# Order of the softmax steps in the attention loops: the copy of the turned probabilities moves between an item's maximum and its reciprocal

## The reference

```python
s = jnp.einsum("bhqd,bhkd->bhqk", q, k).astype(jnp.float32) * scale
if sink is not None:
    s = jnp.concatenate([s, sink_col], axis=-1)
p = softmax_f32(s)            # "swa" drops the sink's column behind it
return jnp.einsum("bhqk,bhkd->bhqd", p.astype(v.dtype), v)
```

## Time and profile before

| | |
|---|---|
| median of three runs | 4626.8 us |
| the profiled execution's own time | 4630.47 us |
| its span | 4628.6 us |
| TensorE matmuls busy | 3098.1 us (67%) |
| VectorE busy | 3119.4 us (67%) |
| ScalarE busy | 908.7 us (20%) |
| GpSimd busy | 1507.9 us (33%) |
| mean granted TensorE clock | 0.828 of full speed |

### The profile page before, as it was taken

The page is one execution under the profiler, slowest core; times in us unless marked ns, Lnnn a source line. Parts: engine busy times, 40 slices in busy tenths (PEclk is TensorE's granted clock), DMA queues, the critical chain, the costliest instruction groups (busy, mean ns, idle before and its releaser), DMA issues.

```text
span 4628.6 us, 49133 instructions
## 1 busy us (share of the span) xinstructions
PE 3098.1 (67%) x16352; PEld 1197.2 (26%) x16352; DVE 3119.4 (67%) x8343; ACT 908.7 (20%) x2468; POOL 1507.9 (33%) x1378
## 2 busy tenths in 40 slices
PE   6889898656885544555575787778885555445554
PEld 2455454311321111111121222554431111111111
DVE  1251346878777788777878764634687877877886
ACT  1252312111111111112111111541111111111211
POOL 0000112444434444444443432010344444344443
PEclk8999999978997787777797998997997777777776
DMA  4252315999999999999999997122899999999998
GB/s 142 84 183 73 132 69 232 415 413 405 417 417 395 419 414 404 420 415 403 393 418 404 415 395 272 35 87 77 333 406 403 408 419 411 408 419 411 398 417 341
DMA packets 307838, 1518.48 MB, mean 328 GB/s; under 512 B 26144, under 2 KB 94240, under 8 KB 143744
## 3 DMA queue, kind: packets, MB, share of 16 engines
q0 software_dynamic: 185888, 1347.13, 70.8%
q1 hardware_dynamic: 87616, 133.07, 8.3%
q10 hardware_dynamic: 34080, 35.14, 2.2%
HBM read 1499.03 MB, written 16.20 MB: 327 GB/s over the span
## 4 chain that ended last, share of the span: by engine, by line
DVE 41%; PE 27%; DMA 19%; issue 7%; ACT 4%; POOL 1%; DVEq 1%; SPq 0%; ACTq 0%; POOLq 0%
DMA X<-in_uv_dram,X 17%; DVE X L2018 17%; PE ps L1112 7%; PE ps L579 6%; DVE X L2029 2%; ACT X L1563 2%; DVE X L1919 1%; DVE X L1917 1%; DVE X L1920 1%; DVE X L2025 1%; PE ps L1029 1%; PE ps L1095 1%; PE ps L906 1%; PE ps L794 1%; PE ps L823 1%
## 5 line engine op out<-in xcount | busy, mean ns | idle before, releaser
L1112 PE MATMUL ps<-X 64*64 64x512 f32 x2560 | 1621.3, 766 | 1276.7 <-DVE X L2029 1259.4
L2152 POOL DMA_INDIRECT X<-in_uv_dram,X x1280 | 1426.8, 1115 | 2166.3 <-PE ps L1115 1692.1
L2018 DVE CUSTOM_DVE_ANT_0 X<-yT,X 128x1024 f32<-128x1024 f32 x1280 | 1531.7, 1223 | 319.0 <-DMA X<-in_uv_dram,X 273.6
L1115 PE MATMUL ps<-X 64*64 64x512 f32 x2560 | 1621.6, 766 | 0.0
L1113 PE MATMUL ps<-X 64*64 64x512 f32 x2560 | 1621.5, 766 | 0.0
L1114 PE MATMUL ps<-X 64*64 64x512 f32 x2560 | 1621.5, 766 | 0.0
L1112 PEld LDWEIGHTS ps<-X 64*64 64x64 f32 x2560 | 355.9, 161 | 2444.1 <-DVE X L2029 1752.2
L1563 ACT ACTIVATE X<-X 128x1 f32<-128x1 f32 x1280 | 256.6, 202 | 2282.7 <-DVE X L2018 2224.3
L1115 PEld LDWEIGHTS ps<-X 64*64 64x64 f32 x2560 | 356.3, 161 | 0.0
L1113 PEld LDWEIGHTS ps<-X 64*64 64x64 f32 x2560 | 356.2, 161 | 0.0
L1114 PEld LDWEIGHTS ps<-X 64*64 64x64 f32 x2560 | 356.0, 161 | 0.0
(11 more groups left out here) (288 smaller groups left out, 3597.5 us busy)
## 6 DMA issues: line engine op xcount, KB each, us to landing
wring<-in_ada_w_dram SPq DMA_DIRECT2D x48, 1024.0 KB
wring<-in_w_in_dram SPq DMA_DIRECT2D x36, 1024.0 KB
wring<-in_peer_wq_dram SPq DMA_DIRECT2D x24, 1024.0 KB
X<-in_uv_dram,X POOLq DMA_INDIRECT x1280
wring<-in_w_out_dram SPq DMA_DIRECT2D x8, 1024.0 KB
X<-scores ACTq DMA_DIRECT2D x64, 128.0 KB
X<-mods ACTq DMA_DIRECT2D x15, 512.0 KB, 6.7
ahead<-X ACTq DMA_DIRECT2D x18, 256.0 KB
```

The costliest lines, as they stand in the source:

```text
L1112: pe.matmul(ps[0:HD, h, :], dg(slice(0, HD), s), v0[0:HD], **ends)
L1115: m = pe.matmul(ps[0:HD, 2 + h, :], dg(slice(HD, P), s + 1), v1[HD:P], **ends)
L2018: v.tensor_tensor_reduce(uvr[:, slot, 0:D], h2[:, t, :], uvr[:, slot, 0:D], 1.0, 0.0, ALU.mult, ALU.add, adot[:, s_:s_ + 1]).then_inc(S("d ...
L2152: g.indirect_dma_start(uvr[:, slot, :], None, a["uv"], bass.IndirectOffsetOnAxis(ap=istages[i % 2][:, s:s + 1], axis=0)).then_inc(S(f"uv{s ...
```

## The change

On ScalarE the normalisation that stands behind the exponential of item i is now that of item i itself. On VectorE the reciprocal of a round is now that of item i, too, and it stands behind the copy of item i-2. No instruction is added or taken away, and TensorE's, SyncE's and GpSimd's lists stay as they are.

```diff
@@ ScalarE, attention(kind)
                                                  bias=att[:, 1, c:c + 1], accum_out=att[:, 2, c:c + 1]).then_inc(S("a_exp"), 1)
-                        if 1 <= i <= N:
-                            j = i - 1
-                            w = width(items[j][2])
-                            act.wait_ge(S("a_r"), ab + j + 1)
-                            nc.scalar.activation(pr3[:, j % 3, 0:w], pr3[:, j % 3, 0:w], ACT.Copy, scale=att[:, 5, j % 32:j % 32 + 1]).then_inc(S("a_no"), 1)
+                            act.wait_ge(S("a_r"), ab + i + 1)
+                            nc.scalar.activation(pr3[:, i % 3, 0:w], pr3[:, i % 3, 0:w], ACT.Copy, scale=att[:, 5, c:c + 1]).then_inc(S("a_no"), 1)
                         p = (i - 5) // 2
                         if i >= 5 and i % 2:
                             y_out(p)
@@ VectorE, attention(kind)
-                        if 1 <= i <= N:
-                            c = (i - 1) % 32
-                            total = att[:, 2, c:c + 1]
-                            v.wait_ge(S("a_exp"), ab + i)
-                            if kind == "swa":
-                                link(v.tensor_tensor(att[:, 4, c:c + 1], att[:, 2, c:c + 1], att[:, 3, c:c + 1], ALU.add))
-                                total = att[:, 4, c:c + 1]
-                            v.reciprocal(att[:, 5, c:c + 1], total).then_inc(S("a_r"), 1)
                         if i >= 2:
                             j = i - 2
                             w = width(items[j][2])
...
                             v.tensor_copy(pT4[:, j % 4, 0:w], ps[:, 4:6, :].rearrange("p a b -> p (a b)")[:, 0:w]).then_inc(S("a_pt"), 1)
+                        if i < N:
+                            c = i % 32
+                            total = att[:, 2, c:c + 1]
+                            v.wait_ge(S("a_exp"), ab + i + 1)
+                            if kind == "swa":
+                                link(v.tensor_tensor(att[:, 4, c:c + 1], att[:, 2, c:c + 1], att[:, 3, c:c + 1], ALU.add))
+                                total = att[:, 4, c:c + 1]
+                            v.reciprocal(att[:, 5, c:c + 1], total).then_inc(S("a_r"), 1)
```

## The result

The changed kernel took 4663.2 us (median of four runs, 4657.1 to 4669.15), the kernel before beside it 4628.4 us (four runs). The ratio is 1.0071, with an interval of 1.0058 to 1.0083: slower by 0.7%, or 34.8 us, where the prediction said 22.6. A second measurement of the same text gave 4658.2 us, a ratio of 1.0068 (1.0054 to 1.0081). The direction and the two ties came out as told; the size lay above the range, at the upper end of rival 3 (22.6 + 6 to 12 us).

A forecast was written before the change was run, and what follows sets the result against it. Chains of waits bound the attentions, with TensorE mostly busy only in "mla". Terms of 12.5 us in layer 0 and 10.1 in layer 1 gave 22.6, added to the median 4626.8: 4649 us, range 4639 to 4659.

The forecast's parts named there:

- the two ties: In the attentions: VectorE's next item waits for this item's exponential; `y_out` waits for its own round's normalisation; bounds 4637 to 4678.
- rival 3: Attentions slower still through more low-clock stretches of TensorE: 22.6 + 6 to 12 us, about 4658 us; chance 0.13.
- What bounds the kernel, and that a loss in an attention reaches the end one for one: Six attentions, some 375 us: only TensorE, only in "mla", is mostly busy; TensorE's projections follow, so losses reach the end.
- Tie A in "swa": VectorE's next item waits for this item's exponential: +0.49 us a 640 pair, +2.3 us in layer 1's lead-in.
- Tie A, lead-in of "mla": Layer 1: exponentials 0 and 1 start 2.28 instead of 1.29 us apart, delaying TensorE's second and third scores: +1.0 us.
- Tie B: In "mla", `y_out` waits for its own round's normalisation, TensorE's `values` for `y_out`: +0.42 us a pair, +2.1 layer 1, +2.9 layer 0.
- End of "swa": Layer 1, no scores left: the last but one `values` waits for a later `y_out`, +1.8 us.
- Earlier normalisation costed at nothing: TensorE's 26.7 us of waits before the transposes shrink, counted as no gain; bounds 0 and -26.7 us.
- The clock put at nothing: TensorE's lower clock after idling in "swa" and "na" was left out of the sum; it could add 2 to 5 us.
- two to four slow groups: Further groups of score matmuls at TensorE's low clock, 1.2 us each, together 2 to 5 us.
- the exemption of "mla": The clock gate would slow "swa" and "na" beyond the sum and leave "mla" alone, its granted clock being 1.00 in layer 1.

The follow-up runs named there:

- Experiment 7: The changed kernel with ScalarE's `y_out` moved ahead of the wait for its own round's reciprocal and normalisation: 4648.8 us, ratio 1.0042.
- experiment 3: The changed kernel with ScalarE's order put back as in the kernel before, VectorE's new order kept: 4655.9 us, ratio 1.0058.
- after again: The changed kernel, unchanged, measured and profiled a second time beside the kernel before: 4658.2 us, ratio 1.0068.
- light warming: Kernel before and changed kernel, each with nine extra matmuls in the lead-in of layer 1's "mla": 4632.0 and 4658.4 us, ratios 1.0004 and 1.0058.

## Why the prediction was wrong, step by step

- *What bounds the kernel, and that a loss in an attention reaches the end one for one*: right. The attentions grew by 29.4 and 33.1 us in the two profiles of after, the medians by 34.8 and 30.0.
- *Tie A in "swa"*: right. 0.48 to 0.49 us a pair (forecast 0.49), lead-in 2.3 (2.3).
- *Tie A, lead-in of "mla"*: the second exponential came 0.97 us later (1.0), and the term was right up to there.
- *Tie B*: right. 0.51 or 0.52 us a pair instead of 0.42, because line 823 begins 0.14 us behind the end of `y_out` and not 0.04.
- *End of "swa"*: with lead-in and pairs +6.15 us up to the last but one product, some 5.7 of it by the order, against 5.6.
- *Earlier normalisation costed at nothing*: not quite right, and small where it can be seen. TensorE's 26.7 us of waits went and the time didn't fall, but that says nothing of what the change would have cost without it. Experiment 7 beside experiment 3 gives it up to 0.9 us at an attention's end, which the sum doesn't hold.
- *The clock put at nothing*: **this step failed.** The prediction named the effect, put "two to four slow groups" at 2 to 5 us beside the sum, spoke of "swa" and "na" alone and left "mla" out, and gave rival 3, 6 to 12 us more, a chance of 0.13. The runs show TensorE's busy time 10.5 us longer with the same instructions. In "mla" of layer 1, the stage that the text had exempted, the clock is worth 2.7 us: the stage grew by 5.6 us, and by 2.9 with the clock at 1.00 in both kernels, where the sum said 3.1. In "swa" of layer 1 it is some 1.8 of 7.5 us. 29.4 less 22.6 is 6.8 us, after again 10.5: rival 3's size, and its 4658 is what the second measurement gave.
- What was wrong is the exemption of "mla", made because TensorE idles less there. It fills the steady loop; its lead-in is made of waits, and the change adds one, the 0.71 us between the second and the third scores, which had run on without a gap. The scores behind that wait are the ones that took 2.93 us, at a granted clock of 0.50. As TensorE is the bound right behind it, nothing made up for it. By the Trainium skill ("TensorE: Matmul & The Clock Gate", Part 1, the HAM clock gate) the rate follows how busy the array has been recently; the light warming agrees in the direction (with nine matmuls more, 1.00 instead of 0.94), but experiment 7, with the same list and the same waits up to these scores, had 1.00 too: that the added wait alone brings the fall isn't shown, and TensorE's own list in the stage wouldn't have told.
- *The range*, 4639 to 4659, held the second measurement and not the first. Its upper edge was drawn in the middle of rival 3 (28.6 to 34.6 us, so 4655 to 4661); what lies outside the attentions differed between profiles by another 2 to 4 us.

Of the 6.8 us, the clock's share is thus measured in "mla" and "swa" of layer 1. In "na" of layer 1 the clock was kinder than before: TensorE was busy 2.6 us less, and the stage grew by 0.7 us against a forecast of 1.4. In layer 0 the share is argued from TensorE's longer busy time (1.9 us in "mla", 3.1 in "na").

Left open: why "na" of layer 0 took 61.7 and 61.8 us in two profiles and 64.8 and 66.2 in two others, though its text and all ahead of it is the same, and what decides whether the half-clock piece comes in the lead-in of "mla". Neither could be tied to a step here.

## What to carry to other kernels

When an order of work is made tighter, look for what now stands behind a wait that it didn't stand behind: here an evacuation of 0.35 us behind someone else's normalisation cost 0.5 us a pair, and moving it ahead gave back 9 to 14 us in all, the clock's share included. Price ties from the timeline's starts, which held within 0.1 us a pair here, and then price the clock of every stretch in which the change adds idle time to TensorE, the lead-in of a TensorE-bound loop above all: compare TensorE's busy time at equal counts of instructions. Useless work meant to hold the clock up costs little as long as it is little (nine matmuls, 0.7 us in their stage), but it gained nothing in the whole here, and too much becomes the bound.

## What the runs showed of the hardware

- With equal counts (2287 matmuls in the six stretches) TensorE was busy 282.1 us before and 292.6 us after; the same four score matmuls took 1.56 or 2.93 us, which of the two can differ between two kernels whose TensorE has done the same in that stage.
- With nine extra 128x128 matmuls in its lead-in a stage took 52.3 us at a granted clock of 1.00, without them 54.3 us at 0.94 in two profiles; that the matmuls did it is not shown.
- In "na" of layer 0 the same instructions at the same place took 61.7 to 66.2 us in different executions, once the order had changed, and 59.7 to 59.8 before.
